# The start of a two-block transformer kernel, reordered: loads, condition, first weight slots, first low halves

## The chip, the cores and the metric

The kernel runs on one core of a Trainium2 chip. The metric is the time of one execution on the device in microseconds; smaller is better. The core has TensorE (PE: matrix products from SBUF into PSUM), VectorE (DVE), ScalarE (ACT) and GpSimd (POOL), which run side by side and wait for one another through semaphores, and SyncE (SP), which here only starts transfers.

## What is computed

Two transformer blocks in float32 on 512 tokens of width 1024. The first block attends in two branches and has an MLP; the second has a convolution layer and an attention layer, each followed by a gated MLP. The part that this change touches is the beginning of the first block:

```python
cs = jax.nn.silu(c)
mod = cs @ ada_w[l] + ada_b[l]
shift1, scale1, gate1, shift2, scale2, gate2 = jnp.split(mod, N_MOD, axis=-1)
h = modulate(rmsnorm(x, norm1_g[l]), shift1, scale1)
proj = h @ w_in[l]
qa, ka, va, qb, kb, vb, ga, gb = jnp.split(proj, offsets, axis=-1)
```

## The kernel before

Activations lie transposed in SBUF: 8 tiles of 128 channels x 512 tokens. Every float32 factor of a product is split into a high half, rounded by ScalarE to TensorE's format, and a low half (the rest), made by VectorE or GpSimd; three products (lines 587 to 589: high x high, high x low, low x high) add up to one float32 product. Weights go through *slots* of 128x2048: SyncE loads a slot into one of two buffers `raw`, ScalarE makes its high half in one go (`convert`, line 1046) or in four *pieces* (`piece`, line 1052), and VectorE (line 1417) or, for slots named in `PIECED`, GpSimd (line 1908) the low half. There are two slots of halves (`NW = 2`), so a slot's halves are made when the slot two before it has been used up.

Each engine has its own program, written in order; only semaphores tie them together. In the start (stage 0) SyncE loads the condition `c`, the 8 slices of 1 MB of `ada_t` that give shift and scale of the first norm (three buffers), x in two halves, and the first weight slots. GpSimd's own queue loads the small tables. TensorE multiplies a one-hot table into rows of attention bias (line 805), ScalarE copies them out of PSUM (line 1185), and they go to memory and come back skewed, as tables that each attention head loads (line 1959). VectorE makes silu(c) and sums it against each slice (`ada_sum`, line 1426: two rows of 128x1024 a slice, slices 0 to 3 are shift, 4 to 7 scale). ScalarE squares x (line 1068) and GpSimd adds up the squares (line 2000); TensorE sums over the channels (line 652), ScalarE takes the root (line 1078), VectorE inverts it and builds a diagonal (line 1504), TensorE spreads it over a PSUM bank (line 665). Then for each of 8 tiles k: VectorE multiplies by it (line 1528), ScalarE applies scale and shift (line 1093) and rounds (line 1098), VectorE makes the low half (line 1511). After that come the first jobs: `qa0` and `qa1` (slots 0 and 1), each two jobs of 24 products (8 tiles x 3), ScalarE and VectorE taking the results out of PSUM (lines 1112 and 1542); then `kva` (slot 2), again two jobs of 24, and then the attention. GpSimd clears the key buffers (line 2010) after stage 0 and before the first bias tables.

## Time and profile before

| what | us |
|---|---|
| median of three runs (2074.97, 2075.18, 2080.67) | 2075.18 |
| the profiled execution | 2071.92 |
| its span, first to last instruction | 2070.1 |
| TensorE busy (94% of the span) | 1946.3 |
| VectorE busy (57%) | 1184.6 |
| ScalarE busy (36%) | 754.5 |
| GpSimd busy (16%) | 328.4 |

Engines overlap, so their times don't add up to the span. The engine that is busy nearly all the time bounds the kernel; where it is idle, the chain of waits says for whom.

### The profile page before, as it was taken

The numbers are of one execution on the slowest core, as the hardware profiler recorded it, in microseconds if no ns is written. First come the engines' busy times: TensorE is split into PE (matmuls) and PEld (weight loads), VectorE is DVE, ScalarE is ACT, GpSimd is POOL, SyncE is SP. The second block draws the span as 40 slices with busy tenths as digits, with TensorE's granted clock in tenths as the row PEclk, the third lists the DMA queues.
The fourth block names the chain that finished last, engine by engine and source line by source line (L and its number), as shares of the span: only waits on it lengthen the run. The fifth ranks groups of instructions, "written<-read, shape, count | busy, mean of one in ns | idle before, by whom it ended". The sixth has DMA issues, their size and how long they took to land.

```text
span 2070.1 us, 22436 instructions
## 1 busy us (share of the span) xinstructions
PE 1946.3 (94%) x9050; PEld 1600.6 (77%) x9050; DVE 1184.6 (57%) x1858; ACT 754.5 (36%) x1134; POOL 328.4 (16%) x288
## 2 busy tenths in 40 slices
PE   2999999999999999998999999989999889999996
PEld 1788888778888877886888888758888668888884
DVE  6566555577676745566655644565666554432436
ACT  3566622352222234223422122364565342222223
POOL 3232211021111102003100000147222130000002
PEclk9999999999999999998999999989999989999998
DMA  9512266356565434431554532232111223323321
GB/s 307 149 57 87 73 235 242 101 197 224 210 223 186 160 102 163 143 122 62 210 200 180 183 96 88 83 108 80 62 42 41 67 77 102 101 83 102 102 82 41
DMA packets 126120, 267.55 MB, mean 129 GB/s; under 512 B 4463, under 2 KB 33151, under 8 KB 126016
## 3 DMA queue, kind: packets, MB, share of 16 engines
q1 hardware_dynamic: 121056, 248.59, 34.9%
q0 software_dynamic: 4960, 17.53, 2.4%
q8 instruction: 71, 1.16, 0.2%
q14 instruction: 33, 0.27, 0.0%
HBM read 261.84 MB, written 8.45 MB: 131 GB/s over the span
## 4 chain that ended last, share of the span: by engine, by line
PE 77%; DVE 10%; ACT 7%; issue 2%; POOL 1%; DMA 0%; ACTq 0%; DVEq 0%; POOLq 0%
PE ps L587 24%; PE ps L588 24%; PE ps L589 24%; DVE t L1537 2%; ACT t L1139 2%; DVE t L1571 1%; DVE t L1511 1%; DVE t L1528 1%; ACT t L1052 1%; ACT t L1171 1%; PE ps L702 1%; DVE t L1525 1%; DVE t L1576 1%; ACT t L1093 1%; POOL t L2090 1%
## 5 line engine op out<-in xcount | busy, mean ns | idle before, releaser
L587 PE MATMUL ps<-t 128*128 128x512 f32 (+1 forms) x2584 | 1004.2, 389 | 35.6 <-DVE t L1511 26.1
L589 PE MATMUL ps<-t 128*128 128x512 f32 (+1 forms) x2584 | 995.9, 385 | 0.0
L588 PE MATMUL ps<-t 128*128 128x512 f32 (+1 forms) x2584 | 995.7, 385 | 0.0
L587 PEld LDWEIGHTS ps<-t 128*128 128x128 f32 x2584 | 488.0, 189 | 141.9 <-issue 29.8
L1417 DVE TENSOR_TENSOR t<-t 128x2048 fp32r<-128x2048 f32 x135 | 309.3, 2291 | 463.5 <-ACT t L1046 463.5
L589 PEld LDWEIGHTS ps<-t 128*128 128x128 f32 x2584 | 487.5, 189 | 102.7
L588 PEld LDWEIGHTS ps<-t 128*128 128x128 f32 x2584 | 488.0, 189 | 97.0 <-issue 1.0
L1046 ACT ACTIVATE t<-t 128x2048 fp32r<-128x2048 f32 x135 | 258.1, 1912 | 613.2 <-PE ps L589 608.7
L1426 DVE CUSTOM_DVE_ANT_0 t<-t 128x1024 f32<-128x1024 f32 x160 | 198.5, 1283 | 19.6 <-DMA t<-in_ada_t 12.5
L1474 DVE SCALAR_TENSOR_TENSOR t<-ps,t 128x512 f32<-128x512 f32 x184 | 132.4, 747 | 82.4 <-PE ps L589 74.0
L1537 DVE TENSOR_TENSOR t<-ps,t 64x512 fp32r<-64x512 f32 (+4 forms) x183 | 103.8, 577 | 102.3 <-ACT t L1171 48.7
L1937 POOL COPY t<-t 128x512 f32<-128x512 f32 x4 | 4.0, 1008 | 861.8 <-DVE t L1490 861.8
L1908 POOL TENSOR_TENSOR t<-t 128x512 fp32r<-128x512 f32 x80 | 105.6, 1333 | 218.6 <-ACT t L1052 218.6
L1537 DVE TENSOR_TENSOR t<-t 128x512 fp32r<-128x512 f32 (+1 forms) x93 | 71.3, 768 | 72.0 <-ACT t L1315 30.7
L1139 ACT ACTIVATE t<-t 128x256 f32<-128x256 f32 (+3 forms) x128 | 69.3, 542 | 117.9 <-DVE t L1576 116.7
L2039 POOL TENSOR_TENSOR t<-t 128x512 f32<-128x512 f32 x32 | 45.6, 1426 | 281.9 <-ACT t L1254 281.9
L1068 ACT ACTIVATE t<-t 128x512 f32<-128x512 f32 x56 | 35.1, 631 | 92.7 <-DVE t L1474 77.0
L702 PE MATMUL ps<-t 128*128 128x128 f32 x296 | 53.2, 279 | 13.2 <-DVE t L1537 11.6
L1315 ACT ACTIVATE t<-t 128x512 fp32r<-128x512 f32 x44 | 27.8, 632 | 100.2 <-DVE t L1780 100.2
L1571 DVE CUSTOM_DVE_ANT_0 t<-ps,t 128x256 f32<-128x256 f32 (+3 forms) x128 | 58.4, 456 | 8.9 <-PE ps L690 6.2
L1093 ACT ACTIVATE t<-t 128x512 f32<-128x512 f32 x56 | 45.3, 809 | 36.3 <-DVE t L1528 36.3
L1511 DVE TENSOR_TENSOR t<-t 128x512 fp32r<-128x512 f32 x56 | 47.9, 858 | 17.0 <-ACT t L1098 16.5
(151 smaller groups left out, 1399.0 us busy)
## 6 DMA issues: line engine op xcount, KB each, us to landing
t<-in_ada SPq DMA_DIRECT2D x48, 1024.0 KB, 5.9
t<-in_gate SPq DMA_DIRECT2D x22, 1024.0 KB, 5.1
t<-in_up SPq DMA_DIRECT2D x22, 1024.0 KB, 5.1
t<-in_down SPq DMA_DIRECT2D x22, 1024.0 KB, 5.0
t<-in_w_in SPq DMA_DIRECT2D x17, 1024.0 KB, 5.5
t<-in_w_mlp_in SPq DMA_DIRECT2D x16, 1024.0 KB, 5.3
t<-in_w_mlp_out SPq DMA_DIRECT2D x16, 1024.0 KB, 5.0
t<-in_ada_t POOLq DMA_DIRECT2D x13, 1024.0 KB, 6.1
```

The costliest lines, as they stand in the source:

```text
L587: pe.matmul(o, wh, xh, start=first, stop=False)
L588: pe.matmul(o, wh, xl, start=False, stop=False)
L589: return pe.matmul(o, wl, xh, start=False, stop=last)
L702: ins = pe.transpose(psum[bank][:, blocks[n]], sp_b[h % 2][:, col:col + P], ident)
L1046: act.activation(WH[:, n % NW, :], raw[:, n % NRAW, :], ACT.Copy).then_inc(w_hi.sem, w_hi.up("slot", n))
L1139: act.activation(prob(st, h, i), prob(st, h, i), ACT.Exp, bias=neg[:, i:i + 1], accum_out=sm[:, i:i + 1]).then_inc(a_exp.sem, a_exp.up("ex ...
L1417: dve.tensor_tensor(WL[:, n % NW, :], raw[:, n % NRAW, :], WH[:, n % NW, :].bitcast(F), ALU.subtract).then_inc(w_lo_d.sem, w_lo_d.up("slot ...
L1426: ins = dve.tensor_tensor_reduce(out=v, in0=v, in1=csb[which][:, :], scale=1.0, scalar=0.0, op0=ALU.mult, op1=ALU.add, accum_out=mods[:, c ...
L1474: return dve.scalar_tensor_tensor(out=X[k], in0=psum[bank][:, :], scalar=gate, in1=X[k], op0=ALU.mult, op1=ALU.add)
L1537: dve.tensor_tensor(lo, src, hi.bitcast(F), ALU.subtract).then_inc(d_lo.sem, d_lo.up(*event))
L1571: dve.tensor_tensor_reduce(out=prob(st, h, i), in0=psum[bank][:, 0:n], in1=bias_of(st, h, i), scale=1.0, scalar=LOW, op0=ALU.add, op1=ALU. ...
L1908: pool.tensor_tensor(WL[:, n % NW, s], raw[:, n % NRAW, s], WH[:, n % NW, s].bitcast(F), ALU.subtract).then_inc(w_lo_p.sem, w_lo_p.up("slo ...
```

## The change

The first loads go out in another order, and each of the 8 slices has a buffer of its own: condition, slices 0 and 4, x, weight slot 0, slices 1 and 5, slot 1, the bias rows, the other four slices, slot 2. The names are buffers: t15 to t17 (and from t18 on) hold slices, t1 is x, t2 the raw weights. SyncE's queue from its start, before:

```order
L2157 DMA t6<-in_c_b 128x1024
L2141 DMA t15<-in_ada_t 128x2x1024
L2141 DMA t16<-in_ada_t 128x2x1024
L2141 DMA t17<-in_ada_t 128x2x1024
L2162 DMA t1<-in_x_t 128x4x512 x2
L2166 DMA bias_rows<-t26 16x1024
L2141 DMA t15<-in_ada_t 128x2x1024
L2141 DMA t16<-in_ada_t 128x2x1024
L2141 DMA t17<-in_ada_t 128x2x1024
L2141 DMA t15<-in_ada_t 128x2x1024
L2128 DMA t2<-in_w_in 128x8x256
```

and now:

```order
L2219 DMA t6<-in_c_b 128x1024
L2205 DMA t15<-in_ada_t 128x2x1024
L2205 DMA t19<-in_ada_t 128x2x1024
L2224 DMA t1<-in_x_t 128x4x512 x2
L2192 DMA t2<-in_w_in 128x8x256
L2205 DMA t16<-in_ada_t 128x2x1024
L2205 DMA t20<-in_ada_t 128x2x1024
L2192 DMA t2<-in_w_in 128x8x256
L2232 DMA bias_rows<-t31 16x1024
```

The weight loads and x have moved ahead of most slices, and the bias-row store behind both of the first weight slots.

silu(c) is kept in two banks of PSUM, and `ada_sum` reads it there; ScalarE copies it back to SBUF later. The adds of the norm's squares go from GpSimd to VectorE. The modulation columns are finished in pairs (`two_columns`), each as soon as its shift slice and its scale slice are summed, and the modulation of tile k waits only for its pair. VectorE's program around the first multiplications by the norm (`t<-t,ps` 128x512), before (from the last of the 16 sums, ISA, on):

```order
L1426 ISA t<-t 128x1024
L1426 ISA t 128x1
L1450 TENSOR_TENSOR t<-t 128x16
L1417 TENSOR_TENSOR t<-t 128x2048
L1455 SCALAR_TENSOR_TENSOR t<-t 128x8
L1457 COPY t<-t 128x8
L1528 TENSOR_TENSOR t<-t,ps 128x512 x2
L1511 TENSOR_TENSOR t<-t 128x512
L1528 TENSOR_TENSOR t<-t,ps 128x512
```

and now, from the diagonal on:

```order
L1535 TENSOR_SCALAR t<-t 128x128 x4
L1673 TENSOR_TENSOR t<-t,ps 128x512 x2
L1457 ISA t<-t,ps 128x1024
L1457 ISA t 128x1
L1457 ISA t<-t,ps 128x1024
L1457 ISA t 128x1
L1673 TENSOR_TENSOR t<-t,ps 128x512 x2
L1457 ISA t<-t,ps 128x1024
L1457 ISA t 128x1
L1457 ISA t<-t,ps 128x1024
L1457 ISA t 128x1
L1665 TENSOR_TENSOR t<-t 128x2
```

The sums now stand between the multiplications, the 128x2048 low half of a weight slot and the 128x512 low halves are gone from here.

Weight slots 0 and 1 are made in pieces (after the squares, and after tile 3), and GpSimd makes their low halves and those of the 8 tiles. GpSimd's program from its last small load to the first bias tables, before:

```order
L1993 DMA t<-in_hot 33x1024
L2000 ISA
L2000 TENSOR_TENSOR t<-t 128x512 x7
L2010 MEMSET t 64x2x512 x8
L1959 DMA t<-skew 128x256 x2
```

and now (L1967 is `piece`, L2055 the low half of a tile):

```order
L2052 DMA t<-in_hot 33x1024
L1967 ISA
L1967 TENSOR_TENSOR t<-t 128x512 x4
L2055 TENSOR_TENSOR t<-t 128x512 x4
L1967 TENSOR_TENSOR t<-t 128x512 x4
L2055 TENSOR_TENSOR t<-t 128x512 x4
L2074 MEMSET t 64x2x512 x8
L2018 DMA t<-skew 128x256 x2
```

The seven adds have gone, and the order slot 0, tiles 0 to 3, slot 1, tiles 4 to 7, then the clearing, is fixed.

TensorE multiplies slots 0 and 1 side by side, in four PSUM banks: tiles 0 to 3 of slot 0, tiles 0 to 3 of slot 1, tiles 4 and 5 of slot 0, 4 of slot 1, 6 and 7 of slot 0, 5 to 7 of slot 1.

```diff
@@ -60,6 +60,10 @@
...
+QA_BANKS = [(6, 7), (0, 4)]
@@ -168,7 +172,7 @@
...
-PIECED = set(range(4, 12)) | set(range(AT_FOX + 3, AT_O + 2)) | {
+PIECED = {0, 1} | set(range(4, 12)) | set(range(AT_FOX + 3, AT_O + 2)) | {
     s + 1 for s in (AT_MLP, AT_CONV, AT_FFN, AT_Q, AT_LAST)}
@@ -332,8 +336,10 @@
...
-for _j in range(ADA_STREAM):
-    ADA_BUF[_j] = ("start", _j % 3)
+FIRST_ADA = [_j + 4 * _w for _j in range(4) for _w in range(2)]
+for _j in FIRST_ADA:
+    ADA_BUF[_j] = ("start", _j)
@@ -345,7 +351,8 @@
...
-        psum = [ctx.enter_context(nc.psum_tensor(f"ps{i}", [P, T], F)) for i in range(8)]
+        banks = ctx.enter_context(nc.psum_tensor("ps", [P, 8 * T], F))
+        psum = [banks[:, T * i:T * (i + 1)] for i in range(8)]
@@ -366,7 +373,7 @@
...
-            ada_mem["start"] = [sb(ph, [2048], F)[:, :] for _ in range(3)]
+            ada_mem["start"] = [sb(ph, [2048], F)[:, :] for _ in range(8)]
@@ -438,6 +445,7 @@
...
+        cs_first = banks[:, T:3 * T]
@@ -544,15 +553,18 @@
...
-            return ada_in["pool" if part == "branch" else "sp"][i]
+            return ada_first[i] if part == "start" else ada_in["pool" if part == "branch" else "sp"][i]
+        def lows_of(name):
+            return p_lo if name == "h1" else d_lo
@@ -801,20 +813,25 @@
...
-            for i, (c0, n) in enumerate(((0, 512), (512, 128), (640, 384))):
-                pe.matmul(psum[i][0:16, 0:n], tb33[0:33, :], hot[0:33, c0:c0 + n], start=True, stop=True).then_inc(
+            for i, bank in enumerate((0, 4)):
+                pe.matmul(psum[bank][0:16, :], tb33[0:33, :], hot[0:33, T * i:T * (i + 1)], start=True, stop=True).then_inc(
                     mm.sem, mm.up("row", i))
-                freed[i] = [(a_evac, ("row", i))]
+                freed[bank] = [(a_evac, ("row", i))]
+            freed[1] = freed[2] = [(a_evac, ("cs", 1)), (d_ada, ("sum", 7))]
             on.wait_ge(cst_in, "landed")
-            norm_finish("n1", False, p_sum, "times")
...
-            for c, name in enumerate(("qa0", "qa1", "kva")):
-                n = take("B", "w_in", 0, 256 * c)
-                for i in range(2):
-                    for u in range(8):
-                        job_unit(name, n, i, u, 6 + i, "h1")
+            for c in range(3):
+                take("B", "w_in", 0, 256 * c)
+            for n, us in ((0, (0, 1)), (0, (2, 3)), (1, (0, 1, 2, 3)), (0, (4, 5)), (1, (4,)), (0, (6, 7)), (1, (5, 6, 7))):
+                for u in us:
+                    for i in range(2):
+                        job_unit(f"qa{n}", n, i, u, QA_BANKS[n][i], "h1")
+            for i in range(2):
+                for u in range(8):
+                    job_unit("kva", 2, i, u, 6 + i, "h1")
@@ -1048,7 +1065,8 @@
...
-                on.wait_ge(mm, "slot", n - NW)
+                if n >= NW:
+                    on.wait_ge(mm, "slot", n - NW)
                 act.activation(WH[:, n % NW, s], raw[:, n % NRAW, s], ACT.Copy).then_inc(w_hi.sem, w_hi.up("slot", n, c))
@@ -1058,12 +1076,12 @@
...
-                m, adder = norm_mem[site], p_sum if site == "n1" else d_norm
+                m = norm_mem[site]
...
-                    on.wait_ge(adder, "acc", site, k - 2)
+                    on.wait_ge(d_norm, "acc", site, k - 2)
                 dst = m["sq"][(k - 1) % 2] if k else m["acc"]
                 act.activation(dst, X[k], ACT.Square).then_inc(a_norm.sem, a_norm.up(site, "sq", k))
@@ -1089,7 +1107,7 @@
...
-                    on.wait_ge(d_lo, *order[at - len(bufs)])
+                    on.wait_ge(lows_of(name), *order[at - len(bufs)])
@@ -1179,25 +1197,35 @@
...
-            act.activation(ada_mem["start"][0][:, 0:D], csb[0][:, :], ACT.Sigmoid).then_inc(a_norm.sem, a_norm.up("silu", 0))
-            for i, (c0, n) in enumerate(((0, 512), (512, 128), (640, 384))):
+            act.activation(ada_mem["start"][7][:, 0:D], csb[0][:, :], ACT.Sigmoid).then_inc(a_norm.sem, a_norm.up("silu", 0))
+            for i, bank in enumerate((0, 4)):
                 on.wait_ge(mm, "row", i)
-                act.activation(rrow[0:16, c0:c0 + n], psum[i][0:16, 0:n], ACT.Copy).then_inc(a_evac.sem, a_evac.up("row", i))
+                act.activation(rrow[0:16, T * i:T * (i + 1)], psum[bank][0:16, :], ACT.Copy).then_inc(
+                    a_evac.sem, a_evac.up("row", i))
             on.wait_ge(d_cols, "eps")
             for k in range(KT):
                 square("n1", k, x_in[k // 4], "landed")
+            for c in range(4):
+                piece(0, c)
             root("n1", False, rmse)
-            convert(0)
-            normed("n1", "h1", cA, cB, ("fold", "h1"), norm_mem["n1"]["tm"])
-            at_end("act", 0, a_hi)
-            take(1)
+            for k in range(KT):
+                modulate("n1", "h1", k, X[k], cA, cB, ("fold", "h1", k // 2), HH)
+                if k == 3:
+                    for c in range(4):
+                        piece(1, c)
+            on.wait_ge(d_ada, "sum", 7)
+            for i in range(2):
+                act.activation(csb[0][:, T * i:T * (i + 1)], cs_first[:, T * i:T * (i + 1)], ACT.Copy).then_inc(
+                    a_evac.sem, a_evac.up("cs", i))
+            at_end("act", 0, a_evac)
+            slot[0] = 1
...
             for n in range(2):
                 for i in range(2):
-                    evacuate(f"qa{n}", n, i, 6 + i)
+                    evacuate(f"qa{n}", n, i, QA_BANKS[n][i])
                 take(1)
@@ -1421,9 +1449,12 @@
...
+                if j >= ADA_STREAM and not which:
+                    on.wait_ge(a_evac, "cs", 1)
+                cs = cs_first if j < ADA_STREAM else csb[which][:, :]
                 for i in range(2):
                     v = ada_buffer(j)[:, i * D:(i + 1) * D]
-                    ins = dve.tensor_tensor_reduce(out=v, in0=v, in1=csb[which][:, :], scale=1.0, scalar=0.0, op0=ALU.mult,
+                    ins = dve.tensor_tensor_reduce(out=v, in0=v, in1=cs, scale=1.0, scalar=0.0, op0=ALU.mult,
                                                    op1=ALU.add, accum_out=mods[:, col + i:col + i + 1])
@@ -1619,24 +1650,52 @@
...
-            silu(0, ada_mem["start"][0])
             dve.memset(tb33[32:33, :], NEG).then_inc(d_cols.sem, d_cols.up("neg"))
-            for j in range(6):
+            on.wait_ge(a_norm, "silu", 0)
+            for i in range(2):
+                s = slice(T * i, T * (i + 1))
+                ins = dve.tensor_tensor(cs_first[:, s], csb[0][:, s], ada_mem["start"][7][:, s], ALU.mult)
+            ins.then_inc(d_ada.sem, d_ada.up("silu", 0))
+            def two_columns(j):
+                s, r = slice(2 * j, 2 * j + 2), slice(8 + 2 * j, 10 + 2 * j)
+                on.wait_ge(vec_in, "landed")
+                on.wait_ge(d_ada, "sum", 4 + j)
+                dve.tensor_tensor(cB[:, s], mods[:, s], vec[:, s], ALU.add)
+                dve.tensor_tensor(mods[:, r], mods[:, r], vec[:, r], ALU.add).then_inc(d_cols.sem, d_cols.up("mod", "scale", j))
+                on.wait_ge(d_cols, "mod", "scale", j)
+                dve.scalar_tensor_tensor(out=cA[:, s], in0=mods[:, r], scalar=1.0, in1=vec8("norm1_g")[:, s], op0=ALU.add,
+                                         op1=ALU.mult).then_inc(d_cols.sem, d_cols.up("fold", "h1", j))
+            def times(*ks):
+                for k in ks:
+                    dve.tensor_tensor(X[k], X[k], psum[5][:, :], ALU.mult).then_inc(d_norm.sem, d_norm.up("n1", "times", k))
+            ada_sum(0)
+            ada_sum(4)
+            two_columns(0)
+            for k in range(1, KT):
+                add("n1", k)
+            diagonal("n1", False)
+            on.wait_ge(mm, "n1", "rs")
+            times(0, 1)
+            ada_sum(1)
+            times(2, 3)
+            ada_sum(5)
+            two_columns(1)
+            times(4, 5, 6, 7)
+            for j in (2, 3):
                 ada_sum(j)
-            diagonal("n1", False)
-            for j in (6, 7):
-                ada_sum(j)
-            mod_bias(0, 16, VCOL["ada_b"])
-            convert(0)
-            fold("h1", cA, cB, 0, 1, vec8("norm1_g"), None, 0)
-            normed("n1", "h1", tm=norm_mem["n1"]["tm"])
-            at_end("dve", 0, d_lo)
-            take(1)
+                ada_sum(4 + j)
+                two_columns(j)
+            at_end("dve", 0, d_cols)
+            slot[0] = 1
@@ -1991,20 +2050,25 @@
...
-            m = norm_mem["n1"]
...
+            def low(k):
+                on.wait_ge(a_hi, "h1", k)
+                pool.tensor_tensor(HH[1][:, k, :], norm_buffers("n1")[k % 2], HH[0][:, k, :].bitcast(F), ALU.subtract).then_inc(
+                    p_lo.sem, p_lo.up("h1", k))
+            for c in range(4):
+                piece(0, c)
+            for k in range(4):
+                low(k)
+            for c in range(4):
+                piece(1, c)
+            for k in range(4, KT):
+                low(k)
+            at_end("pool", 0, p_lo)
...
-            on.wait_ge(p_sum, "acc", "n1", 7)
+            on.wait_ge(p_lo, "h1", 7)
@@ -2136,7 +2200,7 @@
...
-                elif j == 0:
+                elif j == 7:
                     on.wait_ge(d_ada, "silu", 0)
@@ -2146,8 +2210,6 @@
...
-                    if n == 0:
-                        load(2)
@@ -2155,20 +2217,22 @@
...
             sp.dma_start(csb[0][:, :], a["c_b"]).then_inc(c_in[0].sem, c_in[0].up("landed", by=16))
-            for j in range(3):
-                ada_load(j)
+            ada_load(0)
+            ada_load(4)
             for hf in range(2):
                 k0 = 4 * hf
                 sp.dma_start(x_t[:, k0:k0 + 4, :], a["x_t"][k0 * P:(k0 + 4) * P, :].rearrange("(kt p) n -> p kt n", p=P)).then_inc(
                     x_in[hf].sem, x_in[hf].up("landed", by=16))
-            for i in range(3):
+            load(0)
+            ada_load(1)
+            ada_load(5)
+            load(1)
+            for i in range(2):
                 on.wait_ge(a_evac, "row", i)
             sp.dma_start(table, rrow[0:16, :]).then_inc(rows_out.sem, rows_out.up("stored", by=16))
-            for j in (3, 4, 5, 6):
+            for j in FIRST_ADA[4:8]:
                 ada_load(j)
-            load(0)
-            ada_load(7)
-            load(1)
+            load(2)
```

## Rows read from the trace of the kernel before

**Rows 1.** Windows: busy us (xcount) by engine, granted clock, DMA share, GB/s

```profile
10.00:20.00 10.00, 0.90 (x2) 0.00 (x0) 7.14 (x12) 1.05 (x3) 0.00 (x0) 1.00 1.02 404
47.30:57.90 10.60, 8.76 (x25) 5.10 (x26) 8.29 (x13) 10.41 (x14) 0.67 (x1) 1.00 0.53 128
57.90:85.30 27.40, 27.36 (x121) 22.34 (x119) 10.93 (x9) 7.40 (x10) 8.04 (x10) 1.00 0.81 221
```

**Rows 2.** Chain of waits in the start: start us, length us, what

```profile
33.88 1.85 PE ps L652 x8
35.75 0.27 ACT t L1078
...
41.92 2.20 DVE t L1417
```

**Rows 3.** Timeline of TensorE: start us, length us, line, operation [idle before]

```profile
36.60 2.07 PE L665 MATMUL ps<-t 128*128 128x128 f32 x8 [0.89 <-DVE t L1504]
```

**Rows 4.** Timeline of ScalarE in the start

```profile
4.16 1.06 ACT L1182 ACTIVATE t<-t 128x1024 f32<-128x1024 f32 x1 [2.13 <-DMA t<-in_c_b]
...
10.94 0.48 ACT L1185 ACTIVATE t<-ps 16x384 f32<-16x384 f32 x1 [0.96 <-PE ps L805]
19.42 1.67 ACT L1068 ACTIVATE t<-t 128x512 f32<-128x512 f32 x3 [8.01 <-DMA t<-in_x_t]
...
24.13 1.28 ACT L1063 ACT_TABLE_LOAD   x1
...
44.97 0.81 ACT L1093 ACTIVATE t<-t 128x512 f32<-128x512 f32 x1 [6.40 <-DVE t L1528]
45.81 0.63 ACT L1098 ACTIVATE t<-t 128x512 fp32r<-128x512 f32 x1
...
74.42 0.60 ACT L1112 ACTIVATE t<-ps 128x512 fp32r<-128x512 f32 x1 [4.84 <-PE ps L589]
```

**Rows 5.** DMA issues of three moments: at 4.6, at 65.4 and at 116.8 us

```profile
t<-in_hot POOLq DMA_DIRECT2D x1, 132.0 KB, 2.6
...
t<-skew POOLq DMA_DIRECT2D x2, 128.0 KB, 9.7
...
t<-skew POOLq DMA_DIRECT2D x1, 128.0 KB, 5.6
```

**Rows 6.** Timeline of VectorE in the start

```profile
25.93 2.28 DVE L1426 CUSTOM_DVE_ANT_0 t<-t 128x1024 f32<-128x1024 f32 x1
...
36.26 0.87 DVE L1504 TENSOR_SCALAR t<-t 128x128 f32<-128x128 f32 x4
37.05 1.22 DVE L1426 CUSTOM_DVE_ANT_0 t<-t 128x1024 f32<-128x1024 f32 x1
...
44.19 1.27 DVE L1528 TENSOR_TENSOR t<-t,ps 128x512 f32<-128x512 f32 x2
...
76.85 2.29 DVE L1417 TENSOR_TENSOR t<-t 128x2048 fp32r<-128x2048 f32 x1 [1.11 <-ACT t L1046]
```

**Rows 7.** Timeline of VectorE in the attention, GpSimd at work beside it

```profile
89.17 0.42 DVE L1571 CUSTOM_DVE_ANT_0 t<-ps,t 128x256 f32<-128x256 f32 x1
...
110.21 1.89 DVE L1589 TENSOR_SCALAR t<-t 128x128 f32<-128x128 f32 x3
```

**Rows 8.** Timeline of GpSimd

```profile
20.73 13.00 POOL L2000 TENSOR_TENSOR t<-t 128x512 f32<-128x512 f32 x7 [15.59 <-ACT t L1068]
57.23 7.87 POOL L2010 MEMSET t<- 64x1024 f32 x8 [23.50 <-ACT t L1098]
...
89.72 3.80 POOL L1908 TENSOR_TENSOR t<-t 128x512 fp32r<-128x512 f32 x3 [23.20 <-ACT t L1052]
```

**Rows 9.** Timeline of TensorE after two other idle times

```profile
418.51 0.77 PE L587 MATMUL ps<-t 128*128 128x512 f32 x1 [3.16 <-DVE t L1511]
...
1653.68 0.50 PE L587 MATMUL ps<-t 128*128 128x512 f32 x1 [2.91 <-DVE t L1417]
```

**Rows 10.** Window with the first of these, columns as in rows 1

```profile
413.50:423.20 9.70, 6.54 (x19) 5.34 (x20) 5.78 (x11) 6.91 (x11) 2.57 (x2) 0.50 0.01 2
```

More of the change, by code:

```diff
@@ L534, in build @@
         ada_in = {p: signals(f"ada_{p}0_landed ada_{p}1_landed ada_{p}2_landed") for p in ("sp", "pool")}
+        ada_first = signals(" ".join(f"ada_first{i}_landed" for i in range(8)))
         c_in = signals("c_landed c2_landed")
@@ L591, in of_h @@
             def of_h(site):
-                return lambda k: (HH[0][:, k, :], HH[1][:, k, :], [(d_lo, (site, k))])
+                return lambda k: (HH[0][:, k, :], HH[1][:, k, :], [(lows_of(site), (site, k))])
             def of_tile(t, name, *more):
@@ L743, in job_unit @@
                     for kt in (2 * (u % 4), 2 * (u % 4) + 1):
-                        on.wait_ge(d_lo, site, kt)
+                        on.wait_ge(lows_of(site), site, kt)
                         ins = mm3(o, HH[0][:, kt, tok], HH[1][:, kt, tok], hi[:, kt, :], lo[:, kt, :], kt == 0, kt == 7)
                 else:
-                    on.wait_ge(d_lo, site, u)
+                    on.wait_ge(lows_of(site), site, u)
                     ins = mm3(psum[bank][:, :], hi[:, u, blocks[i]], lo[:, u, blocks[i]], HH[0][:, u, :], HH[1][:, u, :],
@@ L1637, in program_dve @@
+            two_columns(1)
+            times(4, 5, 6, 7)
+            for j in (2, 3):
+                ada_sum(j)
+                ada_sum(4 + j)
+                two_columns(j)
+            at_end("dve", 0, d_cols)
+            slot[0] = 1
             for n in range(2):
                 for i in range(2):
-                    evacuate(f"qa{n}", i, 6 + i)
+                    evacuate(f"qa{n}", i, QA_BANKS[n][i])
                 take(1)
@@ L1993, in program_pool @@
             pool.dma_start(hot[0:33, :], a["hot"]).then_inc(hot_in.sem, hot_in.up("landed", by=16))
-            m = norm_mem["n1"]
-            on.wait_ge(a_norm, "n1", "sq", 0)
-            for k in range(1, KT):
-                on.wait_ge(a_norm, "n1", "sq", k)
-                if k > 1:
-                    on.wait_ge(p_sum, "acc", "n1", k - 1)
-                pool.tensor_tensor(m["acc"], m["acc"], m["sq"][(k - 1) % 2], ALU.add).then_inc(
-                    p_sum.sem, p_sum.up("acc", "n1", k))
-            at_end("pool", 0, p_sum)
+            def low(k):
[11 more added lines that the diff above has]
+            at_end("pool", 0, p_lo)
             stage_end(on, 0, "pe", "act", "dve")
             on.wait_ge(rows_out, "stored")
-            on.wait_ge(p_sum, "acc", "n1", 7)
+            on.wait_ge(p_lo, "h1", 7)
             for i in range(2):
```

9 lines of the change are left out of this document (5 added, 4 removed).

## The prediction

> **What bounds the kernel now.** I read the engine totals first: TensorE is busy in 94% of the span, so a prologue in which it stands idle is one of the few places where time can lie. The windows of the start show that place. Between 47.3 and 57.9 us TensorE works on the first job's 24 products with holes, and from 57.9 to 85.3 us it is busy for 27.36 of 27.4 us while five more jobs of 24 products go through: 27.4/120 = 0.228 us a product [rows 1]. Whatever brings the end of the fourth job forward moves all that follows. The chain of waits says why the first job starts so late: after the eight column sums (33.88 us) it runs through VectorE's modulation sums and the 2.20 us low half of the first weight slot at 41.92 [rows 2], both ahead of the first normalised tile. The timelines by engine give the lengths below.
>
> **The change step by step.** I build the new start forward in time, since each step waits for one of two or three others.
>
> *Loads.* The condition is in at 4.16 us [rows 4] and later loads stream at 404 GB/s [rows 1], 2.6 us for 1 MB. In the new order slices 0 and 4 and the two halves of x follow it at once; with about 1 us for the small tables that GpSimd's queue loads meanwhile, the first half of x is there by 4.16 + 3 x 2.6 + 1 = 13.0 us, not 19.42 [rows 4]. Weight slot 0 follows by 18 us, slot 1 by 26 us: neither is waited for below. The bias-row store, now behind slot 1, has no reader until ScalarE's first evacuation.
>
> *The bias rows are the new first gate.* ScalarE copies them out before it squares x; that ended at 10.94 + 0.48 = 11.42 us [rows 4], while it waited for x anyway. Now x comes early, and the rows depend on the one-hot table, the last small load of GpSimd's queue. It landed in 2.6 us on a quiet queue; one load issued while SyncE's queue was moving megabytes took 5.6 us, a pair of others 9.7 us each [rows 5]. The new queue is full from the start, so I add 3.0 us (the 5.6 us row; like the new case it has plain 1 MB loads ahead of it) and keep +0.6 and +7.1 us as bounds. ScalarE squares from 14.4 us.
>
> The Trainium skill, DMA: Bandwidth & Descriptors, section Queues, rings and completion order, says that each DMA engine takes packets from its queues in turn; by that the table would come some 0.6 us late (an estimate), and the sum would be limited by x at 13.0 us and end 1.4 us earlier. The 9.7 us row does not look like taking turns, so I stay with the row between.
>
> *Norm.* Three squares take 1.67 us, the table load for the root 1.28 us [rows 4], an add on VectorE about 0.64 us (two 128x512 rows in 1.27 us [rows 6]). The pairs run in lockstep: add 2 ends at +2.5, square 4 at +3.2, table and root end at +4.7, square 5 at +5.3, add 5 at +6.0, add 7 at +7.4, so 21.8 us. The sums on TensorE take 1.87 us as at 33.88 to 35.75 [rows 2, 3], so the root is at 23.8, and the diagonal starts 0.5 us later as at 36.26 [rows 6], at 24.3. There the last broadcast product ended 2.4 us after that start (36.60 + 2.07 [rows 3]). Now GpSimd converts slot 0 beside it. Three such VectorE rows that met GpSimd's work took 1.89 us [rows 7], where four undisturbed take 0.87 [rows 6], so 1.2 us too long. GpSimd has two pieces left then; bounds 0 and 2.5, taken 1.2. The broadcast is ready at 27.9 us (before: 38.67).
>
> *Modulation.* The first ScalarE step starts 0.78 us after the first multiplication (44.19 to 44.97 [rows 4, 6]), so at 28.7; rounding follows 0.84 us later, a step costs ScalarE 1.4 us (0.81 + 0.63 less the overlap [rows 4]). GpSimd's low half takes 1.27 us (3.80/3, the same operation on a tile of the same size [rows 8]). VectorE goes on: two multiplications until 29.2, slice 1 until 31.6, two until 32.9, slice 5 until 35.3, three short column steps until 35.8. A slice is two rows of 1.22 us [rows 6]. That such a row takes 2.28 us beside GpSimd [rows 6] should not come back: the second operand is now in PSUM, and the PSUM form at 89.17 took 0.42 us for 256 columns while GpSimd was at work [rows 7, 8]; the later 1024-column form I take as 1.2 us, bounds 1.2 and 2.3. Steps 2 and 3 wait for these columns: they start at 35.85 and 37.25, the low half of step 3 ends at 40.0, ScalarE's four pieces of slot 1 at 40.8, GpSimd's at 40.0 + 4 x 1.27 = 45.1 us.
>
> *Products.* Four steps of slot 0 (24 products) are done by then in the holes. From 45.2 us there are 72 products, 16.4 us, without a hole if low halves 4 to 7 are in time. Slices 2 and 6 end at 43.2, the column steps, held up by GpSimd, at 44.5, slices 3 and 7 at 49.3; the last low half is there at 54.0 and needed at 57.9. TensorE has idled some 4 us before the 72. After 3.16 us idle the product at 418.51 took 0.77 us, and up to 423.2 us the granted clock was 0.50, 1.2 instead of 2.4 GHz; after 2.91 us idle the one at 1653.68 took 0.50, with no such stretch [rows 9, 10]. Half speed over 4.7 us loses some 2.3 us; I take 1.7, bounds 0 and 2.3. The fourth job ends at 63.3 us.
>
> *A new wait.* Slot 2 may be rounded only when slot 0 is used up, and that is now 18 products (4.1 us) before the end of the fourth job, at 59.2. From such an end to the low half TensorE needs, before, 74.4 to 76.85 + 2.29 = 79.14, 4.75 us [rows 4, 6]. So kva starts at 64.0, not 63.3: 0.7 us lost. Behind the waiting product stand only kva and the attention. In the profile before, kva started at 74.4. **Gain: 74.4 - 64.0 = 10.4 us.**
>
> *At nothing*: the shared PSUM tensor, one wider row product instead of two, the copy of the condition back to SBUF (two 0.6 us ScalarE rows after the last modulation, before 55 us), the column arithmetic in pairs. GpSimd's clearing and its first bias loads start after the last low half: it cleared from 57.23 to 65.1 [rows 8], so now 54.7 to 62.6, and the loads land by 62.9 + 9.7 = 72.6 at worst; the first score needs them at about 64.0 + 10.9 + 1.2 = 76.1. That slack of 3.5 us is the cover.
>
> The profiled execution took 2071.92 us, so 2061.5 us for its like; the median shown is 3.3 us above it, and I count from the median: 2075.2 - 10.4 = 2064.8 us.
>
> **The rivals.**
> *Nothing collides* (0.20). The table is hardly late (1.4 us, by the turn-taking above), the diagonal is not held (1.2), the clock stays up (1.7): gain 14.7, 2060.5 us. For it speaks the row at 1653.68; against it the loads beside a full queue.
> *PSUM does not free the sums* (0.14). Each of the rows beside GpSimd then takes 1.05 us more and GpSimd's pieces 1.86 instead of 1.27 us (13.00/7 [rows 8]). One sum row beside the first low halves and the eight beside slot 1's pieces delay the last low half to 63.4; 1.4 us of products and 4.75 us of slot 2 follow, kva starts at 69.6: gain 4.8, 2070.4 us. Against it stands the 0.42 us row.
> *The other side: small loads starve* (0.08). If GpSimd's loads wait until SyncE's queue is empty, the one-hot table comes behind slot 1, at 4.16 + 8 x 2.6 = 25.0 us, the rows 4.2 us later at 29.2 instead of 14.4. All of the above moves by 14.8 us: 4.4 us slower, 2079.6 us. It decides from a table 10.4 us later than I take it, at 20.4 us. The 9.7 us row speaks for it in kind; that these two loads did land before SyncE's long store ended speaks against the whole of it.
> *Not passed on* (0.08). If clearing and bias loads come later than the 3.5 us of cover, the attention starts on them: clearing after a last low half delayed as in the second rival would cost some 6 us of the gain: 2070 us.
>
> **How the numbers follow.** The forecast has 0.50; alone it spans 2061 to 2069 us (queue 7.1 - 3.0 = 4.1 us up, clock, diagonal and queue 4.3 down). From 2058 to 2073 us lie forecast, first, second and fourth rival, with some 2 us for the spread of medians (the three runs span 5.7 us); what is left out is the third rival and tails, under 2 in 10. Faster by over 0.3% means under 2069.0 us (0.3%, 6.2 us, is about what this measurement can tell from no change): 0.47 + 0.20 + 0.09 from the edges of two rivals = 0.76. Slower means over 2081.4 us: half of the third rival, 0.04. The rest, 0.20, is within.
>
> **What would show it.** The bias rows leave ScalarE near 14 us and the squares start right behind; the broadcast products end near 28; sum rows stay near 1.2 us beside GpSimd; a hole of about 4 us before the second slot's first product near 45, half-length speed after it; kva's first product near 64 behind a short wait for VectorE's 2.29 us row; everything after kva as before, only earlier. Wrong would be squares after 20 us, sum rows of 2.3 us, a hole inside the 72 products or a wait on the bias loads before the first score.

## The result and the profile after

| | median us | runs |
|---|---|---|
| before, same chip | 2076.31 | 2074.97 to 2080.67, four runs |
| changed | 2065.57 | 2063.71, 2063.83, 2067.32, 2067.59 |
| forecast | 2064.8 | range 2058 to 2073 |

The ratio is 0.9949, 95% interval 0.9936 to 0.9963, so faster by more than the 0.3% that count here: 10.7 us less than before, where 10.4 were forecast. The profiled execution took 2063.71 us, its span 2061.9 us.

The windows of the changed kernel, cut at the events that answer to [rows 1] (columns as there):

```profile
10.00:20.00 10.00, 3.57 (x4) 0.42 (x4) 5.53 (x11) 5.42 (x10) 0.00 (x0) 1.00 1.06 373
33.30:46.30 13.00, 9.22 (x25) 6.66 (x25) 12.86 (x25) 4.91 (x9) 8.69 (x7) 0.87 1.06 300
46.20:63.60 17.40, 16.61 (x72) 13.44 (x72) 8.60 (x16) 10.84 (x16) 12.75 (x13) 1.00 0.93 232
63.60:74.90 11.30, 11.18 (x48) 8.93 (x48) 4.83 (x5) 2.97 (x4) 1.12 (x2) 1.00 0.66 209
```

From 10 to 20 us ScalarE, which mostly waited for x before (1.05 us of work [rows 1]), is now at work for 5.4 us; VectorE, which summed slices for 7.1 us of that window before, is at work for 5.5. From 46.2 us the 72 products of the two slots fill TensorE, and the third slot (`kva`) follows at 63.6. Before, its first product started at 74.2; the 74.4 of the prediction is the start of the evacuation beside it.

ScalarE's timeline of the changed kernel, answering to [rows 4] (L1203 copies bias rows, L1086 squares, L1096 is the root, L1111 a modulation, L1233 the first evacuation of `vt`, 11 us into slot 2):

```profile
14.68 0.59 ACT L1203 ACTIVATE t<-ps 16x512 f32<-16x512 f32 x1 [1.12 <-PE ps L817]
15.17 1.65 ACT L1086 ACTIVATE t<-t 128x512 f32<-128x512 f32 x3
...
24.92 0.26 ACT L1096 ACTIVATE t<-ps,t 128x4 f32<-128x4 f32 x1 [0.87 <-PE ps L664]
30.30 0.82 ACT L1111 ACTIVATE t<-t 128x512 f32<-128x512 f32 x1 [5.12 <-DVE t L1673]
...
37.06 0.82 ACT L1111 ACTIVATE t<-t 128x512 f32<-128x512 f32 x1 [3.91 <-DVE t L1668]
...
74.83 0.60 ACT L1233 ACTIVATE t<-ps 128x512 f32<-128x512 f32 x1 [4.23 <-PE ps L601]
```

The squares start right behind the second row copy, so the bias rows are the first gate, as predicted. The evacuation in the last row stood at 85.30 us before: 10.47 us earlier.

VectorE's timeline, answering to [rows 6, 7] (L1535 is the diagonal, L1457 a sum row, L1665 and L1668 two-column steps, L1445 the low half of slot 2):

```profile
25.43 2.75 DVE L1535 TENSOR_SCALAR t<-t 128x128 f32<-128x128 f32 x4
...
30.72 1.21 DVE L1457 CUSTOM_DVE_ANT_0 t<-t,ps 128x1024 f32<-128x1024 f32 x1
...
36.60 0.16 DVE L1665 TENSOR_TENSOR t<-t 128x2 f32<-128x2 f32 x1
...
41.62 1.21 DVE L1457 CUSTOM_DVE_ANT_0 t<-t,ps 128x1024 f32<-128x1024 f32 x1
...
44.01 1.00 DVE L1665 TENSOR_TENSOR t<-t 128x2 f32<-128x2 f32 x1
...
45.11 1.11 DVE L1668 SCALAR_TENSOR_TENSOR t<-t 128x2 f32<-128x2 f32 x1
...
61.27 2.29 DVE L1445 TENSOR_TENSOR t<-t 128x2048 fp32r<-128x2048 f32 x1 [1.11 <-ACT t L1063]
```

GpSimd's, answering to [rows 8] (L1967 pieces, L2055 low halves of tiles, L2018 the loads of bias tables):

```profile
22.57 5.12 POOL L1967 TENSOR_TENSOR t<-t 128x512 fp32r<-128x512 f32 x4 [17.45 <-ACT t L1070]
31.86 2.65 POOL L2055 TENSOR_TENSOR t<-t 128x512 fp32r<-128x512 f32 x2 [4.16 <-ACT t L1116]
38.62 2.65 POOL L2055 TENSOR_TENSOR t<-t 128x512 fp32r<-128x512 f32 x2 [4.11 <-ACT t L1116]
41.22 4.99 POOL L1967 TENSOR_TENSOR t<-t 128x512 fp32r<-128x512 f32 x4
...
52.84 2.65 POOL L2055 TENSOR_TENSOR t<-t 128x512 fp32r<-128x512 f32 x2 [2.36 <-ACT t L1116]
...
63.81 1.13 POOL L2018 DMA_DIRECT2D t<-skew  x2 [0.30 <-POOL t L2074]
```

GpSimd is at its first pieces while VectorE builds the diagonal, which takes 2.75 instead of 0.87 us [rows 6]. It is at the second slot's pieces while VectorE runs the sum row at 41.62, which takes 1.21 us. That is what the condition in PSUM was priced on.

TensorE's, answering to [rows 3, 9] (the first product behind each hole, and the one behind it):

```profile
33.27 0.76 PE L599 MATMUL ps<-t 128*128 128x512 f32 x1 [3.79 <-POOL t L2055]
...
39.93 0.64 PE L599 MATMUL ps<-t 128*128 128x512 f32 x1 [2.06 <-POOL t L2055]
...
46.26 0.50 PE L599 MATMUL ps<-t 128*128 128x512 f32 x1 [1.72 <-POOL t L1967]
46.60 0.40 PE L600 MATMUL ps<-t 128*128 128x512 f32 x1
...
63.61 0.50 PE L599 MATMUL ps<-t 128*128 128x512 f32 x1 [0.74 <-DVE t L1445]
...
407.95 0.76 PE L599 MATMUL ps<-t 128*128 128x512 f32 x1 [3.16 <-DVE t L1542]
...
1644.13 0.59 PE L599 MATMUL ps<-t 128*128 128x512 f32 x1 [2.90 <-DVE t L1445]
```

The wait for slot 2 at 63.61 is 0.74 us long (forecast 0.7) and ends on VectorE's low half, as forecast. The hole before the second slot, at 46.26, is 1.72 us long, where some 4 us were forecast. The product behind 3.16 us of idle takes 0.76 us again, where [rows 9] had it at 418.51; the one behind 2.90 us takes 0.59 now and had taken 0.50 before [rows 9].

Loads of the first 70 us in the changed kernel, answering to [rows 5] (KB, us from issue to landing):

```profile
t<-in_hot POOLq DMA_DIRECT2D x1, 132.0 KB, 6.4
...
t<-skew POOLq DMA_DIRECT2D x2, 128.0 KB, 5.6
```

The one-hot table took 6.4 us, not 5.6; the bias tables, issued at 63.81, were there by 70, ahead of the `vt` evacuation, and nothing waited for them.

### The profile page after: what moved, and what is told of

It reads as the page before. It is cut to its first block, busy times and chain, and to the rows that moved or that the text cites. A ratio compares the mean times of both kernels' runs of the same rounds, so it can differ in the third digit from the quotient of the medians.

```text
span 2061.9 us, 22454 instructions
## 1 busy us (share of the span) xinstructions
PE 1948.4 (94%) x9048; PEld 1601.6 (78%) x9048; DVE 1180.6 (57%) x1865; ACT 755.6 (37%) x1141; POOL 335.9 (16%) x297
## 4 chain that ended last, share of the span: by engine, by line
PE 66%; DVE 6%; ACT 4%; issue 1%; ACTq 0%; DVEq 0%
PE ps L599 21%; PE ps L601 21%; PE ps L600 21%; DVE t L1568 1%; DVE t L1542 1%; DVE t L1559 1%; DVE t L1556 1%; ACT t L1157 1%; PE ps L714 1%; DVE t L1602 1%; ACT t L1063 1%; DVE t L1513 1%; ACT t L1111 1%; DVE t L1505 0%; PE ps L677 0%
## 5 line engine op out<-in xcount | busy, mean ns | idle before, releaser
L599 PEld LDWEIGHTS ps<-t 128*128 128x128 f32 x2584 | 488.5, 189 | 139.0 <-issue 25.4
L1445 DVE TENSOR_TENSOR t<-t 128x2048 fp32r<-128x2048 f32 x133 | 305.7, 2298 | 461.8 <-ACT t L1063 461.8
L601 PEld LDWEIGHTS ps<-t 128*128 128x128 f32 x2584 | 488.0, 189 | 103.0
L600 PEld LDWEIGHTS ps<-t 128*128 128x128 f32 x2584 | 488.2, 189 | 97.9 <-issue 1.0
L1457 DVE CUSTOM_DVE_ANT_0 t<-t 128x1024 f32<-128x1024 f32 x144 | 175.5, 1260 | 9.7 <-DMA t<-in_ada 4.1
L1967 POOL TENSOR_TENSOR t<-t 128x512 fp32r<-128x512 f32 x88 | 115.9, 1330 | 227.0 <-ACT t L1070 227.0
L1086 ACT ACTIVATE t<-t 128x512 f32<-128x512 f32 x56 | 34.9, 630 | 82.6 <-DVE t L1505 78.6
L1111 ACT ACTIVATE t<-t 128x512 f32<-128x512 f32 x56 | 45.3, 809 | 45.4 <-DVE t L1559 29.9
L714 PEld LDWEIGHTS ps<-t 128*128 128x128 f32 x296 | 37.2, 142 | 25.2 <-DVE t L1568 15.1
```

The costliest lines, as they stand in the source:

```text
L599: pe.matmul(o, wh, xh, start=first, stop=False)
L600: pe.matmul(o, wh, xl, start=False, stop=False)
L601: return pe.matmul(o, wl, xh, start=False, stop=last)
L714: ins = pe.transpose(psum[bank][:, blocks[n]], sp_b[h % 2][:, col:col + P], ident)
L1445: dve.tensor_tensor(WL[:, n % NW, :], raw[:, n % NRAW, :], WH[:, n % NW, :].bitcast(F), ALU.subtract).then_inc(w_lo_d.sem, w_lo_d.up("slot ...
L1457: ins = dve.tensor_tensor_reduce(out=v, in0=v, in1=cs, scale=1.0, scalar=0.0, op0=ALU.mult, op1=ALU.add, accum_out=mods[:, col + i:col + i ...
```

## The experiments

Seven of them change one thing of the changed kernel, two are the changed kernel again, and the last has three edits together. Eight ran once, on two chips: sbuf_sums, serial, slices_first and dve_lows on one, the other four on another. Where an effect is small, two executions of one kernel differ by more than it, so these runs are judged by three marks in the trace: the start of the squares, the first product of slot 1 (behind GpSimd's last piece) and the first product of slot 2.

From the squares to slot 1 the changed kernel took 31.09, 31.11 and 31.10 us in its three traces (the first profile, after_again, after_timed), so differences of some tenths count there. From the squares to slot 2 it took 48.44, 49.82 and 50.04 us; after_again below shows why. Sbuf_sums and serial end 12 and 10 us later than after_again, more than their marks differ by. Their granted clock over the span was 0.974 and 0.973, against 0.978, so their full times aren't used here.

| run | us (before beside it) | squares | slot 1 | slot 2 |
|---|---|---|---|---|
| changed, first profile | 2063.71 | 15.17 | 46.26 | 63.61 |
| after_again: unaltered | 2063.96 (2074.62) | 15.24 | 46.35 | 65.06 |
| sbuf_sums | 2076.10 (2078.59) | 15.68 | 51.63 | 71.01 |
| serial | 2074.40 (2078.59) | | | 68.2 |
| slices_first | 2077.71 (2078.59) | 29.14 | 60.26 | 77.61 |
| dve_lows | 2062.78 (2078.59) | 14.86 | 46.45 | 65.27 |
| tables_first | 2063.11 (2074.62) | 13.87 | 44.97 | 63.86 |
| hold_pieces | 2063.68 (2074.62) | 15.81 | 45.30 | 64.26 |
| early_slice | 2064.27 (2074.62) | 15.68 | 44.58 | 63.37 |

(Serial's order has no such hole before slot 1, and none before slot 2; its last mark is its `vt` evacuation at 79.39, less the 11.2 us that lie between the two in the first profile: an estimate.)

**The condition in SBUF again** (sbuf_sums): silu(c) stays in its SBUF buffer, and a sum has two SBUF operands. ScalarE's copy back is cut to one column, since nothing is to be copied.

```diff
...
-                cs = cs_first if j < ADA_STREAM else csb[which][:, :]
+                cs = csb[which][:, :]
...
```

> One part undone: silu(c) stays in SBUF, so the modulation sums read two SBUF operands again. Theory (the PSUM operand is what keeps VectorE's sums at 1.21 us beside GpSimd): the sum rows that lie beside GpSimd's low halves and slot-1 pieces take 2.2 to 2.3 us again, GpSimd's four slot-1 pieces take 7 to 8 us instead of 4.99, the last low half of a tile comes near 62 us instead of 55.5, and kva's first product starts at 68 to 70 us instead of 63.6. Rival (PSUM does not matter, the sums of the changed kernel are fast because they seldom meet GpSimd): rows of at most 1.3 us, kva at 63.6 +- 0.5 us.

VectorE in this run, beside GpSimd's four pieces from 43.69 to 51.58:

```profile
42.52 2.30 DVE L1457 CUSTOM_DVE_ANT_0 t<-t 128x1024 f32<-128x1024 f32 x1
...
44.75 2.29 DVE L1457 CUSTOM_DVE_ANT_0 t<-t 128x1024 f32<-128x1024 f32 x1
```

The same row that took 1.21 us takes 2.30, and GpSimd's pieces take 7.89/4 = 1.97 us instead of 1.25. Counted from the squares, the second slot's first product comes 4.8 us later than in after_again and slot 2 5.5 us later: the theory holds, and the 69.6 us of the prediction's second rival was a little low (71.01). The Trainium skill, SBUF — State Buffer, section Who interferes with whom, says that a VectorE instruction with two SBUF inputs contends with a GpSimd instruction that reads SBUF, and one with at most one SBUF input, outside VectorE's two-port modes, does not. The sum rows of these two runs agree: 2.30 against 1.21 us. One SBUF input alone is not enough, though: the rows of the diagonal read one 128x128 tensor from SBUF, with a column of scalars, and were held up by GpSimd (2.75 us; hold_pieces below).

**Slot 0 whole, then slot 1** (serial).

```diff
-            for n, us in ((0, (0, 1)), (0, (2, 3)), (1, (0, 1, 2, 3)), (0, (4, 5)), (1, (4,)), (0, (6, 7)), (1, (5, 6, 7))):
+            for n, us in ((0, range(8)), (1, range(8))):
```

> One part undone: all eight tiles of slot 0 are multiplied before slot 1, in the same four PSUM banks. Theory (side by side fills the time in which tiles 4 to 7 are not ready): TensorE waits for the low halves at 49.2, 50.5, 54.2 and 55.5 us, slot 0 ends near 56.9, the 48 products of slot 1 end at 67.8 us or up to 2 us later if the clock falls in the holes; slot 2 is then ready, and kva starts at 67.8 to 69.8 us, 4 to 6 us later than in the changed kernel. Rival (the wait on slot 2 decides, not the products): kva at 63.6 +- 0.5 us.

```profile
49.52 0.80 PE L599 MATMUL ps<-t 128*128 128x512 f32 x1 [4.80 <-POOL t L2055]
```

TensorE stands for 4.80 us before tile 4's low half, with slot 1's products ready but behind it in the program. In this order there was no wait for slot 2, and slot 2 came 3.1 us later than in after_again, at 68.2, within the 67.8 to 69.8 us expected. That is what the side-by-side order is worth.

**All slices ahead of x** (slices_first): so that x comes behind eight of them, where it came behind three before the change and behind two after.

```diff
-            ada_load(0)
-            ada_load(4)
+            for j in (0, 4, 1, 5, 2, 6, 3, 7):
+                ada_load(j)
...
```

The loads of the other six slices further down are taken out.

> One part undone: all eight modulation slices are loaded ahead of x and of the weight slots, everything else as in the changed kernel. Theory (x must come early because squares, adds and broadcast are the path): eight slices at 2.6 us behind the condition (4.2 us) plus 1.5 us of small loads put the first half of x at about 29 us instead of 13.8, the squares start 14 us later than 15.2, and kva's first product comes at 76 to 79 us instead of 63.6, later than in the kernel before (74.4). Rival (the load order only matters while VectorE waits for slices, since VectorE could now sum the slices early): VectorE's program order is fixed, but if it regained time the loss would be under 8 us, kva before 71.5 us.

ScalarE in this run:

```profile
14.38 0.59 ACT L1203 ACTIVATE t<-ps 16x512 f32<-16x512 f32 x1 [1.12 <-PE ps L817]
29.14 1.67 ACT L1086 ACTIVATE t<-t 128x512 f32<-128x512 f32 x3 [14.17 <-DMA t<-in_x_t]
```

The rows leave at 14.97, but the squares wait for x until 29.14, 14.0 us later than in the first profile, and slot 2 starts 14.0 us later. The time at which x is there is passed on one for one. Before the change the squares started at 19.42 [rows 4], so with the rest of the change in place the order of the loads is worth some 4.2 us (an estimate, 19.42 - 15.17, by this exchange).

**The tiles' low halves on VectorE** (dve_lows).

```diff
         def lows_of(name):
-            return p_lo if name == "h1" else d_lo
+            return d_lo
```

with VectorE's `low("n1", "h1", k)` between its multiplications and sums, and GpSimd's taken out.

> One part undone: VectorE makes the low halves of the eight tiles again (0.69 us each), GpSimd only the pieces of slots 0 and 1. Theory (GpSimd's low halves save VectorE 5.5 us of a program that is nearly full, though each takes 1.33 us instead of 0.69): slot 1's low halves come near 47.0 us (46.2 in the changed kernel), the last tile's low half near 58.3 instead of 55.5 us, and kva starts 1 to 2 us later, at 64.6 to 65.6 us. Rival (the shorter VectorE operation is the better one, since only single tiles are waited for): kva at or before 63.6 us.

By the marks, counted from the squares, slot 1 starts 0.5 us later and slot 2 0.6 us later than in after_again. I had expected 1 to 2 us; that slot 2's 65.27 lies within the 64.6 to 65.6 us expected is chance, since after_again has 65.06 without this edit. What GpSimd is spared, VectorE takes on, so this part of the change is worth about half a microsecond here.

**The changed kernel again** (after_again).

> The changed kernel once more, unaltered. The start was 10.5 us earlier at the first score in the profiled execution, but only 8.2 us were left at its end. If the 2.3 us lost in between come from the change, kva to the end takes about 1998.3 us here again (1995.7 us in the kernel before); if they are spread between executions, kva's first product is again at 63.6 +- 0.3 us and the rest differs from 1998.3 by over 1 us.

TensorE in this execution:

```profile
40.01 0.50 PE L599 MATMUL ps<-t 128*128 128x512 f32 x1 [1.21 <-POOL t L2055]
...
42.67 0.39 PE L601 MATMUL ps<-t 128*128 128x512 f32 x1
46.35 0.80 PE L599 MATMUL ps<-t 128*128 128x512 f32 x1 [3.29 <-POOL t L1967]
46.94 0.63 PE L600 MATMUL ps<-t 128*128 128x512 f32 x1
47.37 0.63 PE L601 MATMUL ps<-t 128*128 128x512 f32 x1
...
49.40 0.39 PE L600 MATMUL ps<-t 128*128 128x512 f32 x1
49.63 0.39 PE L601 MATMUL ps<-t 128*128 128x512 f32 x1
```

Up to 46.35 all is within 0.1 us of the first profile. Then the seven products from 46.35 on start 0.43 us apart, at half the rate of 0.23 that follows. In the first profile it was the products from 39.93 on that went at half rate, ahead of a hole of 1.72 us that hid it. Here the hole is 3.29 us and the loss lies behind it: 7 x 0.20 = 1.4 us, and slot 2 starts 1.45 us later. The windows of both show it in the granted clock: 0.87 before and 1.00 after 46.2 us in the first profile, 0.98 and 0.92 in this one:

```profile
33.30:46.30 13.00, 8.51 (x24) 5.91 (x24) 12.86 (x25) 4.87 (x8) 8.78 (x7) 0.98 1.07 303
46.30:65.10 18.80, 18.01 (x73) 14.51 (x73) 8.64 (x16) 10.88 (x16) 13.90 (x14) 0.92 0.83 209
```

So the clock's 1.7 us of the forecast come and go between executions of one kernel.

Neither branch of what I expected came true as written: kva started at 65.06, not at 63.6 +- 0.3, and from there to the end it took 1997.1 us, between the 1998.3 of the first profile and the 1995.7 of the kernel before.

**Bias tables first on GpSimd's queue** (tables_first).

```diff
+            pool.dma_start(tb33[0:32, :], a["rel_bias"]).then_inc(tab_in.sem, tab_in.up("landed", by=16))
+            pool.dma_start(hot[0:33, :], a["hot"]).then_inc(hot_in.sem, hot_in.up("landed", by=16))
             pool.dma_start(cst[:, 0:2 * P], a["consts"][:, 0:2 * P]).then_inc(cst_in.sem, cst_in.up("ones", by=16))
...
```

The two loads are taken out where they stood, at the end of the small tables.

> GpSimd's queue loads the bias table and the one-hot table ahead of its other small tables. Theory (the bias rows gate the squares): the one-hot table, landed at 11.0 us in the changed kernel, lands at 7 to 8 us, the rows leave ScalarE before 12 us, the squares start with x at 13.9 instead of 15.2 us, and kva starts 1.3 us earlier, at 62.3 us. Rival (x or the adds gate): squares at 13.9 us, but kva within 0.3 us of 63.6.

```profile
12.08 0.59 ACT L1203 ACTIVATE t<-ps 16x512 f32<-16x512 f32 x1 [1.12 <-PE ps L817]
13.87 1.67 ACT L1086 ACTIVATE t<-t 128x512 f32<-128x512 f32 x3 [1.20 <-DVE t L1666]
```

The rows leave ScalarE at 12.67, not before 12 as expected, and the squares now start 1.2 us later, behind another gate. VectorE's L1666, which the trace names for that wait, isn't read by them; x is, and its first half, issued at 2.2, took 11.6 us to land: 13.8. The table itself still took 6.4 us: going first on its queue didn't make it faster, only earlier. The 1.4 us by which the squares start earlier than in after_again are passed on to slot 1 (44.97 against 46.35).

**GpSimd held until the diagonal is built** (hold_pieces).

```diff
+            on.wait_ge(d_norm, "n1", "diag", 3)
             for c in range(4):
                 piece(0, c)
```

> GpSimd starts the pieces of slot 0 only when VectorE has written the fourth part of the diagonal. Theory (the diagonal took 2.75 us because GpSimd's pieces blocked it): the diagonal takes 0.87 us again, the broadcast ends near 27.6 instead of 29.5 us, slot 1's low halves come near 44.3 instead of 46.2 us, and kva starts near 61.7 us, although GpSimd's first two tile low halves come later. Rival (something else slows the diagonal, or the later pieces of slot 0 cost as much): kva at 63.6 us or later.

```profile
26.07 0.88 DVE L1535 TENSOR_SCALAR t<-t 128x128 f32<-128x128 f32 x4
```

The diagonal is back at 0.88 us. Counted from the squares, slot 1 starts 1.6 us earlier than in after_again, though the pieces themselves come later. So of the 1.9 us that the rows take longer beside GpSimd, 1.6 lay on the path.

**Slice 1 summed ahead of the diagonal** (early_slice), while VectorE waits for the root.

```diff
+            ada_sum(1)
             diagonal("n1", False)
             on.wait_ge(mm, "n1", "rs")
             times(0, 1)
-            ada_sum(1)
```

> VectorE sums slice 1 between the adds and the diagonal, where it waits 2.3 us for the root, instead of between the multiplications. Theory (VectorE's order, not TensorE or the loads, sets slot 1's low halves by way of the second column pair): the second pair is ready near 34.8 instead of 37.0 us, slot 1's low halves near 43.9 instead of 46.2 us, kva near 61.3 us. Rival (the slot-1 pieces wait for the load or for GpSimd): the second pair is earlier, kva stays at 63.6 +- 0.5 us.

Counted from the squares, slot 1 starts 2.2 us earlier. VectorE's column sums for tiles 2 and 3 are thus on the path to slot 1's pieces.

At slot 2, by the numbers as I wrote them, the rivals of these last three runs hold: it came at 63.86, 64.26 and 63.37 us, not at the 62.3, 61.7 and 61.3 expected. I had counted from the 63.61 of the first profile. In these three, as in after_again, the products behind the hole go at half rate, and beside after_again slot 2 comes 1.2 us earlier in tables_first and, counted from the squares, 1.4 us in hold_pieces and 2.1 us in early_slice. The mark at slot 1, which lies ahead of that stretch, shows the theory in all three.

**The three together** (combined), timed in five rounds beside the changed kernel (after_timed).

> The changed kernel, unaltered, timed beside the next one. kva's first product between 63.6 us (second slot's products at full clock) and 65.1 us (a stretch at half clock among them), 10 us or so ahead of the kernel before; ratio to the kernel before 0.9940 to 0.9965.

> Three edits of the changed kernel together: the bias tables first on GpSimd's queue, GpSimd's first pieces only behind the diagonal, slice 1 summed between the adds and the diagonal. If the three delays are separate links of one chain, as I hold, their gains add up: 1.4 + 1.6 + 2.2 = 5.2 us, so the second slot's first product near 41.2 us instead of 46.35, kva near 59.9, and 4 to 5 us less than the changed kernel, about 2060 us. Rival: GpSimd becomes the bound, since its first four pieces now start behind the diagonal and the low halves of the first tiles queue behind them; then the second slot's first product stays at 44 us or later and less than 2 us is gained. Second rival: the loads (slice 7 landed at 38.9, slot 2 at 41.7 us) end last; then the holes of TensorE move behind the last low half or the wait for slot 2 grows beyond 3 us.

| | median us | runs | ratio to before, 95% interval |
|---|---|---|---|
| before | 2074.19 | nine, 2071.32 to 2077.56 | |
| after_timed | 2065.55 | five, 2064.05 to 2067.62 | 0.9955 (0.9941 to 0.9969) |
| combined | 2062.47 | five, 2060.67 to 2063.70 | 0.9940 (0.9927 to 0.9952) |

Combined is 3.1 us faster than the changed kernel, with no overlap of their runs, and less than the 4 to 5 us I expected. Slot 1 starts at 42.76 and slot 2 at 61.74. Its timeline of VectorE, and of GpSimd:

```profile
22.34 1.22 DVE L1457 CUSTOM_DVE_ANT_0 t<-t,ps 128x1024 f32<-128x1024 f32 x1 [0.46 <-DMA t<-in_ada_t]
...
24.84 0.87 DVE L1535 TENSOR_SCALAR t<-t 128x128 f32<-128x128 f32 x4
...
32.09 1.15 DVE L1665 TENSOR_TENSOR t<-t 128x2 f32<-128x2 f32 x1
```

```profile
25.80 4.96 POOL L1967 TENSOR_TENSOR t<-t 128x512 fp32r<-128x512 f32 x4 [20.58 <-DVE t L1535]
30.73 2.49 POOL L2055 TENSOR_TENSOR t<-t 128x512 fp32r<-128x512 f32 x2
35.09 2.66 POOL L2055 TENSOR_TENSOR t<-t 128x512 fp32r<-128x512 f32 x2 [1.88 <-ACT t L1116]
37.71 4.99 POOL L1967 TENSOR_TENSOR t<-t 128x512 fp32r<-128x512 f32 x4
```

Of the 5.2 us only 46.35 - 42.76 = 3.6 came through, and three delays make up the rest. The squares start at 14.14, 0.3 us later than in tables_first. Slice 1 wasn't there when the adds were done (0.46 us of waiting for the load at 22.34), so the diagonal started 24.84, behind the sums, though the root was out at 24.16. And GpSimd, held back, now makes the low halves of tiles 0 and 1 from 30.73 on, just when VectorE's first column step for tiles 2 and 3 comes: 1.15 us instead of 0.16. Together that is 0.3 + 0.5 + 1.0 = 1.8 us, beside the 1.6 that are missing; that the three add up like this is read from the rows and not tested by a run. Neither rival came true as written (slot 1 is ahead of 44 us, and the wait for slot 2 is 0.74 us as before), but the delays are of their kinds: a load, and GpSimd's later start.

after_timed's slot 2 started at 66.00 in its profiled execution, 0.9 us above the 65.1 expected at most: its squares began at 15.96, 0.7 us later than in after_again.

## Why the prediction was right, point by point

**The gate of the bias rows**: right in kind, a term 0.8 us too small. The table took 6.4 us, where I took 5.6 from one row; the squares started at 15.2, not 14.4. Turn-taking of the queues, by which the Trainium skill (DMA: Bandwidth & Descriptors, section Queues, rings and completion order) let me estimate 0.6 us of delay, falls short: the table took 3.8 us longer than on a quiet queue, and 6.4 us again in tables_first, where it went second on its own queue. The rival on the other side, loads that starve until 20.4 us or later, did not come.

**The norm**: 10.3 us from the squares to the diagonal, forecast 9.9 (before, it was 16.8, from 19.42 to 36.26 [rows 4, 6]). **The diagonal**: held up as forecast, by 1.9 us instead of 1.2 (2.75 us in the profile after, 0.88 in hold_pieces). I had taken three rows held in the attention as the measure; here all four met the pieces.

**Sums beside GpSimd**: right, 1.21 us, and sbuf_sums shows what keeps them short. The row from which I took it had been misread: the one at 89.17 ended at 89.59, before GpSimd's first piece at 89.72 [rows 7, 8]. A later row of the kernel before, beside that piece, bears the reading out:

```profile
90.22 0.43 DVE L1571 CUSTOM_DVE_ANT_0 t<-ps,t 128x256 f32<-128x256 f32 x1 [0.37 <-PE ps L686]
```

**Slot 1's first product**: 46.3, forecast 45.2; the squares' 0.8, the norm's 0.4 and the diagonal's 0.7 are too much by 0.8, by which the broadcast and VectorE's column sums were quicker than I had them.

**The clock**: 1.7 taken, 0 in the first profile, 1.4 in after_again. It made up for the late table in the first profile, and that is luck: from slot 1 to slot 2 it took 17.35 us there and in slices_first, and 18.7 to 19.4 us in the eight other runs with this order of products. So the term of 1.7 us is near what most executions pay.

**The wait for slot 2**: 0.7 forecast, 0.74 measured. **Slot 2**: 64.0 forecast; 63.61, 65.06 and 66.00 in the three traces of the changed kernel, so on the whole a little late. **Everything after as before**: nearly. From the `vt` evacuation to the end of the span it was 1984.8 us before (85.30 to 2070.1) and 1987.1 after (74.83 to 2061.9), so 2.3 us of the 10.5 did not reach the end of the profiled execution. The granted clock over the span was 0.980 before and 0.978 after, which is some 83 and 91 us at half speed. after_again gave back only 1.1 us (76.32 to 2062.2) with another set of such stretches. That it is the clock alone is argued from these numbers, not shown by a run. The program behind kva is the same in all these kernels, and from kva's first product to the end it took between 1995.7 us (dve_lows) and 2004 us (serial), so a loss of 2.3 us between two executions says nothing of the change. The medians of the first rounds are 10.7 us apart, those of the later ones (nine runs before, five of after_timed) 8.6: the forecast's 10.4 lies between, and its closeness to the first is in part luck too.

**Which part brought what**: the earlier x some 4 us (the estimate above), the PSUM operand 5.5, the side-by-side order 3, GpSimd's low halves half a microsecond. These, each from a run with one part undone, come to more than 10.4; undone alone, a part may expose a wait that the others have made short, which no run shows. Nor does any run undo the adds on VectorE (part of the norm that went from 16.8 to 10.3 us), the column pairs or the weight slots in pieces, so what these bring is open.

## What to carry to other kernels

Where a prologue has several engines handing work to one another, build it forward in time from measured rows, and ask at each step what runs beside it on VectorE and GpSimd: an operand moved to PSUM halved a row here, and a 0.9 us helper left with SBUF operands beside GpSimd took 1.9 us longer, 1.6 of it on the path. When a big transfer moves forward, look for the small one that now comes last, and put it first on its queue. Gains of single steps add up only as far as their delays really lie one behind the other: of 5.2 us in three edits, 3.6 came through to the second slot and 3.1 to the end.
